# Moving the last convolution tile and the layer norm among the matrix-memory heads, and gating ahead of the convolution's taps

## What is computed

```python
a, g, q, k, v, o, gates = _split_cols(h @ w_in, AB_SIZES)       # 512 512 256 256 512 512 16 columns
u = _dwconv(a * sigmoid(g), conv_w, conv_b)                     # 31 taps along the tokens, 512 channels
u = silu(_layer_norm(u, ln_g, ln_b))                            # over the 512 channels
h_f = _mlstm_chunkwise(q, k, v, ig_f, log_sigmoid(fg_f), ...)   # matrix memory, 4 heads, forward
h_b = the same over flipped tokens                              # and backward
hm = _rms(h_f + h_b) * head_gain * sigmoid(o)                   # over the 128 features of a head
y = concatenate([u, hm]) @ w_out
```

## Time and profile before

| | us |
|---|---|
| median of three executions | 3785.32 (3780.64 to 3786.0) |
| the profiled execution, its own time | 3791.58 |
| its span, from first to last instruction | 3790.3 |
| busy in the span: PE / DVE / ACT / POOL | 3431.9 / 1732.1 / 1276.8 / 923.0 |
| mean granted clock of TensorE | 0.953 |
| HBM traffic | 281.40 MB read, 4.19 MB written |

### The profile page before, as it was taken

One profiled execution on the slowest core, in us unless ns is written; L12 is line 12 of the kernel. 1 busy time (PEld: TensorE's weight loads), 2 busy tenths in 40 slices (PEclk: granted clock), 3 DMA queues, 4 the chain that ended last, 5 costly groups with the idle time before them and its releaser, 6 DMA issues. The chain is left out here.

```text
span 3790.3 us, 44457 instructions
## 1 busy us (share of the span) xinstructions
PE 3431.9 (91%) x17216; PEld 2670.1 (70%) x17216; DVE 1732.1 (46%) x3160; ACT 1276.8 (34%) x2190; POOL 923.0 (24%) x397
## 2 busy tenths in 40 slices
PE   6998998999989898899987787999999898888999
PEld 4765777777766677677766556788898646667887
DVE  4228334534334722543479654522264665544234
ACT  2322323333332232332331442322243446543332
POOL 2112121124302212112322201232264200024443
PEclk9999898999999998999988898999999999999999
DMA  4342012123443202213211100121243110012232
GB/s 147 139 150 83 29 67 76 53 80 114 140 156 127 74 33 68 72 55 107 99 45 50 50 1 28 56 67 56 67 134 100 55 57 1 1 51 82 96 99 80
DMA packets 87907, 288.48 MB, mean 76 GB/s; under 512 B 10000, under 2 KB 20624, under 8 KB 86800
## 3 DMA queue, kind: packets, MB, share of 16 engines
q1 hardware_dynamic: 86688, 275.80, 21.5%
q10 hardware_dynamic: 1008, 9.83, 0.7%
HBM read 281.40 MB, written 4.19 MB: 75 GB/s over the span
## 5 line engine op out<-in xcount | busy, mean ns | idle before, releaser
L394 POOL TENSOR_TENSOR weights_low<-weights_loaded,weights_high 128x1024 fp32r<-128x1024 f32 (+2 forms) x380 | 909.3, 2393 | 2850.5 <-ACT weights_high L376 2815.6
L307 PE MATMUL psum<-h_high,weights_high 128*128 128x512 f32 (+1 forms) x2400 | 924.3, 385 | 71.3 <-DVE h_low L554 26.9
L308 PE MATMUL psum<-h_low,weights_high 128*128 128x512 f32 (+1 forms) x2400 | 894.0, 372 | 0.0
L309 PE MATMUL psum<-h_high,weights_low 128*128 128x512 f32 (+1 forms) x2400 | 892.3, 372 | 0.0
L307 PEld LDWEIGHTS psum<-h_high,weights_high 128*128 128x128 f32 x2400 | 462.3, 193 | 171.4 <-issue 71.6
L376 ACT CAST weights_high<-weights_loaded 128x1024 fp32r<-128x1024 f32 (+2 forms) x380 | 392.6, 1033 | 493.1 <-PE psum L309 452.7
L308 PEld LDWEIGHTS psum<-h_low,weights_high 128*128 128x128 f32 x2400 | 462.9, 193 | 83.3 <-issue 10.0
L309 PEld LDWEIGHTS psum<-h_high,weights_low 128*128 128x128 f32 x2400 | 461.4, 192 | 79.3
L3521 DVE TENSOR_TENSOR act_low<-ffn_act,act_high 128x512 fp32r<-128x512 f32 (+1 forms) x66 | 142.3, 2156 | 138.4 <-ACT act_high L3491 138.3
L307 PE MATMUL psum<-act_high,weights_high 128*128 128x512 f32 (+1 forms) x528 | 187.8, 356 | 8.4 <-DVE act_low L3521 6.2
L308 PE MATMUL psum<-act_low,weights_high 128*128 128x512 f32 (+1 forms) x528 | 187.5, 355 | 0.0
(11 more groups left out here) (436 smaller groups left out, 5099.8 us busy)
## 6 DMA issues: line engine op xcount, KB each, us to landing
weights_loaded<-stream_dram SPq DMA_DIRECT2D x472, 512.0 KB, 3.4
weights_loaded<-stream_dram SPq DMA_DIRECT2D x80, 128.0 KB, 3.3
weights_loaded<-stream_dram SPq DMA_DIRECT2D x24, 384.0 KB, 3.1
weights_loaded<-stream_dram SPq DMA_DIRECT2D x8, 272.0 KB, 2.7
x<-x_dram SPq DMA_DIRECT2D x1, 2048.0 KB, 9.5
arena_mem<-mem_dram ACTq DMA_DIRECT2D x2, 1024.0 KB, 6.1
x<-x_dram ACTq DMA_DIRECT2D x1, 2048.0 KB, 8.1
x_kept_dram<-x ACTq DMA_DIRECT2D x1, 2048.0 KB, 6.9
```

Of the source, the lines that this page charges most:

```text
L307: pe.matmul(out, a.high, b.high, start=start, stop=False)
L308: pe.matmul(out, a.high, b.low, start=False, stop=False)
L309: return pe.matmul(out, a.low, b.high, start=False, stop=stop)
L394: pool.tensor_tensor(self.low[s][:, 0:size], raw[:, 0:size], self.high[s][:, 0:size], ALU.subtract).then_inc(*g.event("weights_low").up(po ...
```

## The change

In the conformer stage, ACT takes the sigmoid of g0 ahead of Exp and Ln of the forget gate, and exponentiates the stack only after q0 and q1 are taken. ACT's copy of a finished tile comes one turn later. DVE gates a tile as soon as its order allows, with the remaining taps of earlier tiles behind: gating 0, one group of taps, the forget chain, two groups, gating 1, six groups, gating 2, six, gating 3, nine. Only tiles 0 to 2 are convolved there, still in banks 6 and 7. POOL fills `up` and `one_row` first.

Tile 3 is convolved in the loop of the heads, one group of taps in each of iterations 0 to 7, and accumulates in SBUF (`t.mixed`) instead of PSUM; `t.up` is kept until then. The layer norm moves from iteration 0 to the end, with `ml_weights[2]` as its scratch instead of `ml_out`. The roots of heads 0, 1 and 2 are taken inside the loop (iterations 4, 6 and 8), each over its own six columns; head 3 follows at the end. `column_root_vector` is cut in two functions with the same instructions. In `mlstm_vector`, `mean(h)` waits for the squares of a head, `normalized(h)` holds the Newton steps and the scaling, and `gained(h)` the gain.

The diff, cut; removed lines of which the new place is shown are left out:

```diff
@@ conformer_scalar
     e = t.gate_tmp[64:128, :]
+    gated(0)
...
-    for m in g.after(act, S("forget").at("rows")):
-        act.wait_ge(*m)
-    act.activation(t.stack[64:128, :], t.gate_max[:, :], ACT.Exp, scale=-1.0).then_inc(*S("stacked").up(act, 0))
-    gated(0)
     for c, one, two in AB_ORDER:
         taken(*one)
         taken(*two)
+        if c == 0:
+            for m in g.after(act, S("forget").at("rows")):
+                act.wait_ge(*m)
+            act.activation(t.stack[64:128, :], t.gate_max[:, :], ACT.Exp, scale=-1.0).then_inc(*S("stacked").up(act, 0))
         gated(c + 1)
         g.weights.round(key(*AB_ORDER[c + 1][1]) if c < 2 else key("v_part", 0, 0))
-        convolved(c)
+        if c:
+            convolved(c - 1)
...
-    convolved(3)
+    convolved(2)
+LATE_CONV, TAPS = 3, 4
@@ conv_vector
-    if j0 == 0:
+    if j0 == 0 and c != LATE_CONV:
...
-            acc = g.banks(6, 2)[:, BANK - CTX + lo:BANK - CTX + lo + n]
+            if c == LATE_CONV:
+                acc = t.mixed[:, c, lo:lo + n]
+            else:
+                acc = g.banks(6, 2)[:, BANK - CTX + lo:BANK - CTX + lo + n]
@@ conformer_vector
+    groups = iter([(c, j) for c in range(LATE_CONV) for j in range(0, CONV_WIDTH, TAPS)])
     def taps(n):
         for _ in range(n):
+            conv_vector(g, *next(groups))
     def gated(c):
-        taps(2)
-        taps(2)
...
     dve.scalar_tensor_tensor(e, fg, -1.0, fg, ALU.mult, ALU.min).then_inc(*S("forget").up(dve, "negated"))
+    gated(0)
+    taps(1)
...
-    gated(0)
-    for c, _, _ in AB_ORDER:
-        convolve(c)
-        taps(2)
-        taps(2)
-        gated(c + 1)
-        taps(8)
-    convolve(3)
-    taps(8)
+    taps(2)
+    gated(1)
+    taps(6)
+    gated(2)
+    taps(6)
+    gated(3)
+    taps(9)
@@ conformer_gpsimd
+    for name, tile, value in (("up", t.up[:, :, :], 0.0), ("one_row", t.one_row[:, :], 1.0),
+                              ("ml_q", t.ml_q[:, :, :], 0.0), ("ml_v", t.ml_v[:, :, :, ML_V:ML_V + 1], 1.0)):
@@ mlstm_tensor
+    def mean():
+        g.claim(key("mean"), 0, 2)
...
+    last = len(ML_TODO)
+    for n in range(last + 1):
+        if n < last:
+            rows_of_head(n)
+        if n >= 1:
+            scores(n - 1)
+        if n >= 2:
+            read(n - 2)
+    mean()
+    read(last - 1)
+    turned(0, 2)
+    turned(1, 4)
+    turned(2, 0)
+    sums_tensor(g, layer_norm(g), Turn(6, 2))
+    turned(3, 2)
@@ mlstm_scalar
+    def root(h):
+        column_root_scalar(g, ("ml", h), *[of_head(t.ml_small[i], h) for i in (2, 0, 1)])
+    last, ln = len(ML_TODO), layer_norm(g)
+    for n in range(last + 1):
+        if n < last:
             exponentials(n)
         if n >= 2 and ML_TODO[n - 2][0] == 1:
             squares(n - 2)
+        if n >= 4 and ML_TODO[n - 4][0] == 0:
+            root(ML_TODO[n - 4][1])
+    squares_scalar(g, ln, [S("drained").at(key("mean"))])
+    squares(last - 1)
+    root(HEADS - 1)
+    root_scalar(g, ln)
+    apply_scalar(g, ln)
@@ mlstm_vector
+    last, ln = len(ML_TODO), layer_norm(g)
+    for n in range(last + 1):
+        if n < last:
             diagonal(n)
+        ended = ML_TODO[n - 4][1] if n >= 4 and ML_TODO[n - 4][0] == 0 else None
+        if ended is not None:
+            mean(ended)
         if n == 0:
+            conv_vector(g, *next(late))
+        if n >= 1:
             scores(n - 1)
+        if 1 <= n < last:
+            conv_vector(g, *next(late))
         if n >= 2:
             read(n - 2)
+        if ended is not None:
+            normalized(ended)
+    for c in range(4):
...
+    squares_vector(g, ln, [])
+    read(last - 1)
+    for h in range(HEADS - 1):
+        gained(h)
+    mean(HEADS - 1)
+    normalized(HEADS - 1)
+    root_vector(g, ln)
+    apply_vector(g, ln)
+    gained(HEADS - 1)
```

More of the change, by code:

```diff
@@ L2347, in conformer_tensor @@
     projected("o", 3)
-    g.owner[6] = g.owner[7] = ("conv", 3)
+    g.owner[6] = g.owner[7] = ("conv", 2)
 def conformer_scalar(g, l):
@@ L2558, in layer_norm @@
     t = g.t
-    hs4 = t.ml_out[:, :, :].rearrange("p t c -> p (t c)").rearrange("p (c n) -> p c n", c=4)
     y = t.mixed[:, 0:4, :]
-    return Norm("layer_norm", y, 4, 0, TOK, lambda c: g.small.ln_g[c], y, hs4, CONV_DIM,
+    return Norm("layer_norm", y, 4, 0, TOK, lambda c: g.small.ln_g[c], y, t.ml_weights[2][:, 0:4, :], CONV_DIM,
                 shift=lambda c: g.small.ln_b[c], func=ACT.Silu)
@@ L2603, in read, with turned @@
         done.then_inc(*S("projected").up(pe, k))
[L2605 to L2620, removed]
+    def mean():
+        g.claim(key("mean"), 0, 2)
+        for lo, hi in BOTH:
+            for c in range(4):
+                for m in g.after(pe, S("convolved").at(LATE_CONV)):
+                    pe.wait_ge(*m)
+                done = mm(g, g.wide(key("mean"), lo, hi), g.ones, t.mixed[:, c, lo:hi], c == 0, c == 3)
+        done.then_inc(*S("projected").up(pe, key("mean")))
+    def turned(h, bank):
         k = key("turned", h)
-        g.claim(k, 2 * (h % 3), 2)
+        g.claim(k, bank, 2)
         for m in g.after(pe, S("ml_normed").at(h)):
@@ L2679, in column_root_scalar, with of_head, column_mean_vector, column_newton_vector @@
     act.activation(out, tmp, ACT.Exp, scale=-0.5).then_inc(*S("root_guess").up(act, key))
-def column_root_vector(g, key, out, x, tmp, dim):
+def of_head(x, h):
+    return x[:, :].rearrange("p (q h) -> p q h", h=HEADS)[:, :, h]
+def column_mean_vector(g, key, x, dim):
     dve, S = g.dve, g.event
     dve.tensor_scalar(x, x, 1.0 / dim, EPS, ALU.mult, ALU.add).then_inc(*S("root").up(dve, (key, "mean")))
+def column_newton_vector(g, key, out, x, tmp):
+    dve, S = g.dve, g.event
     for m in g.after(dve, S("root_guess").at(key)):
@@ L2693, in column_root_vector @@
     dve.scalar_tensor_tensor(out, tmp, 1.5, out, ALU.add, ALU.mult).then_inc(*S("root").up(dve))
+def column_root_vector(g, key, out, x, tmp, dim):
+    column_mean_vector(g, key, x, dim)
+    column_newton_vector(g, key, out, x, tmp)
 def mlstm_vector(g):
@@ L2751, in read, with mean, normalized @@
                     *S("drained").up(dve, k))
[L2753 to L2775, removed]
+    late = iter([(LATE_CONV, j) for j in range(0, CONV_WIDTH, TAPS)])
+    def mean(h):
+        for m in g.after(dve, S("ml_squared").at((h, TT - 1))):
+            dve.wait_ge(*m)
+        column_mean_vector(g, ("ml", h), of_head(t.ml_small[0], h), ML_V)
+    def normalized(h):
+        column_newton_vector(g, ("ml", h), *[of_head(t.ml_small[i], h) for i in (2, 0, 1)])
         r = t.ml_small[2][:, h:h + 1]
-        rsb = bass.AP(tensor=r.tensor, offset=r.offset, ap=[[n, P], [HEADS, TT], [0, ML_V]])
+        rsb = bass.AP(tensor=r.tensor, offset=r.offset, ap=[[TT * HEADS, P], [HEADS, TT], [0, ML_V]])
         hv = t.ml_out[:, :, h * ML_V:(h + 1) * ML_V]
@@ L2781, in mlstm_vector, with gained @@
         dve.tensor_tensor(hv, hv, rsb, ALU.mult).then_inc(*S("ml_normed").up(dve, h))
+    def gained(h):
         k = key("turned", h)
@@ L2786, in mlstm_vector @@
                                  t.mixed[:, HEADS + h, :], ALU.mult, ALU.mult).then_inc(*S("drained").up(dve, k))
+    last, ln = len(ML_TODO), layer_norm(g)
+    for n in range(last + 1):
+        if n < last:
+            diagonal(n)
+        ended = ML_TODO[n - 4][1] if n >= 4 and ML_TODO[n - 4][0] == 0 else None
+        if ended is not None:
+            mean(ended)
+        if n == 0:
+            conv_vector(g, *next(late))
+        if n >= 1:
+            scores(n - 1)
+        if 1 <= n < last:
+            conv_vector(g, *next(late))
+        if n >= 2:
+            read(n - 2)
+        if ended is not None:
+            normalized(ended)
+    for c in range(4):
+        for m in g.after(dve, S("projected").at(key("mean"))):
+            dve.wait_ge(*m)
+        dve.scalar_tensor_tensor(t.mixed[:, c, :], g.wide(key("mean")), -1.0 / CONV_DIM, t.mixed[:, c, :], ALU.mult,
+                                 ALU.add).then_inc(*S("drained").up(dve, key("mean")))
+    squares_vector(g, ln, [])
[7 more added lines that the diff above has]
+    gained(HEADS - 1)
 def ab_out_tensor(g, l, turn):
@@ L3890, in layout_second @@
         t.ml_v = sb("ml_v", [P, TT, HEADS, ML_V + 1], s1)
+        t.up = sb("padded", [P, 4, CTX + SEQ + 4 * PAD], s1)
         t.ml_rows, t.ml_cols = sb("ml_rows", [64, TOK], s1), sb("ml_cols", [P, TT, P], s1)
```

17 lines of the change are left out of this document (removed).

## The result

The changed kernel takes 3753.13 us (median of 7 executions, 3745.59 to 3769.13) against 3785.32 (3780.26 to 3791.53): a ratio of 0.9923, 95% interval 0.9903 to 0.9943. It is 32 us faster, not the 50 of the forecast, and lies 5 us above the range. A second series gave 0.991 (0.9895 to 0.9924). All medians and ratios here are of fast executions, and one of the four of e7_gate_late, at 6873.24 us, is left out.

The account below looks back on a forecast made before the run. It took the first stage to be bound by DVE's order. First stage -39.6 and heads -10.9 (-16.5, +7.4, +2, -3.8) sum to -50.5 us, from the median 3785.32 a forecast of 3735, range 3719 to 3748.

Parts of the forecast that it names:

- First stage: Conformer projections up to the end of o3: 2139.15 becomes 2099.5, so -39.6 us.
- DVE's 9 us wait for the copy behind the cast: After tile 0, DVE goes on 9 us late, as ACT's copy stands behind a cast waiting for a2.
- hole ahead of v: PE wants a3's banks at 2040.1, but DVE gates a3 until 2047.3: a 7.2 us hole and cold start.
- no hole ahead of q1: With the sigmoid of g0 ahead of the logarithm on ACT, PE's 12 us hole before q1 goes.
- Start of the heads: From the fence S to the fourth diagonal: S + 56.3 becomes S + 39.8, so -16.5 us.
- Loop: Matrix-memory heads: five iterations take 73.2 us instead of 65.8, with taps and finished heads' steps on DVE, so +7.4.
- Clock: Loop of the heads: two PE holes of about 3.2 us cost 1 us each in clock, so +2.
- Tail: End of the heads behind the loop, with the layer norm: 45.8 becomes 42 us, so -3.8.
- Taps: Tile 3's groups in the loop: 5.25 us each into SBUF, filling DVE's idle time and overshooting by 1.
- Taps not covered: Rival in the heads' loop: PE's read comes late after taps too, each group costs 5.25; +25, 3760; chance 0.07.
- Heads: Matrix-memory heads from the fence on, start, loop, clock and tail together: -10.9 us.
- cold rival: Rival from the fence on: the L306 matmuls all run at 1.2 GHz; +77, 3812; chance 0.03.

Follow-up runs that it names:

- e7_gate_late: Changed kernel with gating of tile 0 and the sigmoid of g0 back behind the forget chain; ratio 0.994 to the kernel before.
- e6: Changed kernel with tile 3 convolved in the conformer stage again, no taps in the loop; ratio 0.9956 to the kernel before.
- e1: Changed kernel with the mean of a finished head behind DVE's scores instead of ahead; heads 162.74 us, ratio 0.9893 to the kernel before.
- e4: Changed kernel without 24 of tile 3's 31 taps, last group moved to iteration 0; not a correct convolution, traced once; heads 156.83 us.
- e5: Changed kernel with roots and scalings of heads 0 to 2 back behind the loop; heads 159.19 us, ratio 0.9871 to the kernel before.
- b1: Changed kernel with ACT's tile copy ahead of the cast and roots of heads 0 to 2 behind the loop; ratio 0.9869 to the kernel before.
- e3_both: Changed kernel with the mean behind DVE's scores and ACT's tile copy ahead of the cast; 3730.72 us, ratio 0.9853 to the kernel before.

## Why the prediction was right and wrong

- **First stage, right.** -39.6 forecast, -38.8 measured. Each step shows: DVE's 9 us wait for the copy behind the cast (9.00), the hole ahead of v (7.2 forecast, 7.50), no hole ahead of q1. Undoing the parts puts 34.5 us of it on tile 3 (e6) and 10.8 on gating tile 0 ahead of the forget chain (e7); they overlap, since the sum is more than 38.8. No run undoes the earlier gating of tiles 1 to 3 alone.
- **Start of the heads, a term too small.** Forecast S + 39.8, measured 42.4. 0.7 us of it were there at the end of scores 0 (20.7 against about 20). The other 1.8 came in the second scores, which I had taken at full clock: they took 7.1 us instead of 5.3. PE had a hole of 3.68 us ahead of them, and the granted clock behind it was 0.50.
- **Loop, the failed step.** "Every second iteration has the mean, Newton steps and scaling of a finished head besides ... = 1.8": the instructions do take that, but the mean waits for ACT's squares, and those can start only when DVE's own read, the last thing in the iteration before, has ended. DVE meets the wait one diagonal later. 1.77 + 1.77 + 2.77 = 6.3 us, put at nothing in the sum, which e1 takes out. The third stood in the old trace as well (2.77 us ahead of L2684), so the trace could have told.
- **Clock, mis-sized.** I allowed 2 us for two holes of 3.2. There were four of about 4.1 us in the loop, one of 3.68 ahead of it and one of 4.89 in the tail. Only two of the four stand in iterations with a wait for the squares; the other two follow the Newton steps and the scaling, and stay in e1. The loop up to the last read took 82.4 us, forecast 73.2 and 2 for the clock. Of the 9.2 us above 73.2, the two waits are 3.5, slow scores 5.1 (1.0 to 1.5 behind each hole), and 0.5 is a wait ahead of the last read.
- **Tail.** Forecast 42, measured 2260.8 - 2215.7 = 45.1, of which 2.77 is the third wait; the sum of the rest was right within 0.4.
- **Taps, right.** 0.94 us for a group beside PE's read (1 forecast), 5.20 us in SBUF (5.25). "Taps not covered" fell with e4, as far as its 25 us go; the groups after iteration 1 cost 1.5 us on average.
- **The stages behind.** I counted zero; 1 us is real (Silu), and +2.8 was measured with a spread as large.
- **The base.** Taking the sum off the median was right. The profiled executions alone, 3791.58 and 3745.59, would have made the 3741 of the forecast look nearly right, and that would be luck: 10.9 us of their difference lie in code ahead of the change.

Heads: forecast -10.9, measured +1.5, a difference of 12.4 us; with 0.8 from stage one and the 2.8 behind, that is the 16 us between -50.5 and -34.5. Of the cold rival a small share came true: the granted clock was 0.92 over the loop, not 0.50. The runs show holes of 1.2 us without loss and holes of 4.1 us with 1.0 to 1.5 us of loss each. The Trainium skill (TensorE: Matmul & The Clock Gate, section HAM oscillation) says that a burst of matmuls starts at half clock each time when the wait ahead of it is long enough. The trace agrees for the holes of 4.1 us, but the clock was back within the scores or right behind them, so the loop as a whole didn't run cold.

## What to carry over

When work is moved among other work, follow each of its inputs back to the instruction that makes it, also when that is the engine's own last instruction by way of another engine: a mean that costs 0.17 us cost 1.8 to 2.8 for where it stood. An engine that casts ahead in order holds back whatever is queued behind the cast; put the short copy that frees a buffer first. And compare stages from a common event inside both traces, as unchanged code ahead of it moved by up to 15 us here.

## What was not expected

The same program's stages repeat within 0.1 us, while code ahead of them shifts by 4 to 15 us between executions. Heads with the same code (e5, b1) took 159.19 and 162.45 us: in one, the iteration from the fifth diagonal to the sixth takes 14.68 us, in the other 15.63, and from the seventh to the eighth 14.68 and 16.47. In both PE's holes in the loop are 1.5 to 2.5 us. Behind the fifth diagonal the hole is the same (timelines of PE, e5 and then b1):

```profile
2155.19 0.49 PE L306 MATMUL psum<-ml_q,ml_k 128*128 128x128 f32 x2 [2.21 <-DVE ml_weights L2748]
2156.18 2.41 PE L306 MATMUL psum<-ml_q,ml_k 128*128 128x256 f32 x6 [0.50 <-DVE ml_weights L2748]
...
2143.65 0.49 PE L306 MATMUL psum<-ml_q,ml_k 128*128 128x128 f32 x2 [2.21 <-DVE ml_weights L2748]
2144.64 3.36 PE L306 MATMUL psum<-ml_q,ml_k 128*128 128x256 f32 x6 [0.50 <-DVE ml_weights L2748]
```

The granted clock of this iteration was 1.00 in e5 and 0.89 in b1. So a hole of this size sometimes costs clock and sometimes not. What decides it was not tried, nor why the times of the changed kernel spread over 24 us (over 9 in the second series) and those of e3_both over 5.
